# Reading 512 moving columns of the dense products one from each half row in turn, in a two-layer hybrid mixer kernel

## What is computed

```python
def sq_relu_mlp(h, w1, w2):
    return jnp.square(jax.nn.relu(h @ w1)) @ w2
...
for l in range(DEPTH):
    need_ctx = l < DEPTH - 1
    ...
    o_lat, o_ctx = hybrid_mixer(
        modulate(x, norm1_g[l], sh1, sc1), modulate(x_ctx, norm1_g[l], csh1, csc1), w_in[l], ...)
    x = x + g1 * o_lat
    x = x + g2 * sq_relu_mlp(modulate(x, norm2_g[l], sh2, sc2), w_ff1[l], w_ff2[l])
    if need_ctx:
        x_ctx = x_ctx + cg1 * o_ctx
        x_ctx = x_ctx + cg2 * sq_relu_mlp(modulate(x_ctx, norm2_g[l], csh2, csc2), w_ff1[l], w_ff2[l])
return x
```

## Time and profile before

| | |
|---|---|
| median of three executions | 1476.16 us |
| profiled execution | 1476.19 us |
| its span in the trace | 1474.4 us |
| TensorE matmul busy | 1449.2 us, 98% of the span |
| TensorE weight load busy | 1224.4 us, 83% |
| VectorE busy | 939.8 us, 64% |
| ScalarE busy | 645.3 us, 44% |
| GpSimd busy | 209.2 us, 14% |

### The profile page before, as it was taken

How to read it: one execution, slowest core, us unless ns; L and a number is a source line. 1 busy time by engine, 2 the same in 40 slices (tenths; PEclk the granted TensorE clock), 3 DMA queues, 4 the chain that set the end, 5 groups by cost and what they waited for, 6 DMA issues and landing times.

```text
span 1474.4 us, 24978 instructions
## 1 busy us (share of the span) xinstructions
PE 1449.2 (98%) x10474; PEld 1224.4 (83%) x10474; DVE 939.8 (64%) x1479; ACT 645.3 (44%) x969; POOL 209.2 (14%) x172
## 2 busy tenths in 40 slices
PE   8999999999999999999999999999999999999999
PEld 4888777776778888888888888788888779999999
DVE  5777467847445656698655554668378865675564
ACT  5722534364254434542123422562365655564462
POOL 0000001333111110221002200000002611122130
PEclk9999999999999999999999999999999999999999
DMA  9522223023243224256555556042242444455553
GB/s 383 215 87 93 89 95 152 30 98 107 72 186 126 97 86 162 99 197 225 188 190 197 187 202 202 9 144 93 94 158 91 143 137 137 170 210 189 186 197 115
DMA packets 37409, 215.07 MB, mean 146 GB/s; under 512 B 4017, under 2 KB 7729, under 8 KB 13617
## 3 DMA queue, kind: packets, MB, share of 16 engines
q1 hardware_dynamic: 37298, 213.48, 41.1%
HBM read 211.37 MB, written 2.10 MB: 145 GB/s over the span
## 4 chain that ended last, share of the span: by engine, by line
PE 90%; DVE 6%; ACT 2%; issue 1%; DMA 1%; POOL 0%; SPq 0%; DVEq 0%; ACTq 0%
PE ps L1216 11%; PE ps L1215 11%; PE ps L1214 11%; PE ps L591 10%; PE ps L593 10%; PE ps L592 10%; PE ps L814 3%; PE ps L569 2%; PE ps L602 2%; PE ps L603 2%; PE ps L604 2%; DVE arena L2410 1%; DVE parts L2031 1%; PE ps L712 1%; PE ps L796 1%
## 5 line engine op out<-in xcount | busy, mean ns | idle before, releaser
L593 PE MATMUL ps<-parts 128*128 128x512 f32 (+1 forms) x944 | 319.1, 338 | 0.0
L1216 PE MATMUL ps<-parts 128*128 128x512 f32 (+1 forms) x960 | 318.7, 332 | 0.0
L1214 PE MATMUL ps<-parts 128*128 128x512 f32 (+1 forms) x928 | 308.1, 332 | 0.0
L1215 PE MATMUL ps<-parts 128*128 128x512 f32 (+1 forms) x928 | 308.1, 332 | 0.0
L2072 DVE TENSOR_TENSOR parts<-ring,parts 128x1024 fp32r<-128x1024 f32 x124 | 150.1, 1252 | 129.9 <-ACT parts L1582 129.8
L1582 ACT ACTIVATE parts<-ring 128x1024 fp32r<-128x1024 f32 x124 | 124.8, 1053 | 235.9 <-PE ps L1216 228.5
L1216 PEld LDWEIGHTS ps<-parts 128*128 128x128 f32 x960 | 180.2, 188 | 18.6
L593 PEld LDWEIGHTS ps<-parts 128*128 128x128 f32 x944 | 177.2, 188 | 20.4
L591 PE MATMUL ps<-parts 128*128 128x512 f32 (+1 forms) x544 | 189.0, 347 | 0.9 <-ACT arena L1834 0.9
L1215 PEld LDWEIGHTS ps<-parts 128*128 128x128 f32 x928 | 174.2, 188 | 18.2
L1214 PEld LDWEIGHTS ps<-parts 128*128 128x128 f32 x928 | 174.2, 188 | 18.1
(11 more groups left out here) (323 smaller groups left out, 2458.1 us busy)
## 6 DMA issues: line engine op xcount, KB each, us to landing
ring<-in_w_ff SPq DMA_DIRECT2D x64, 1024.0 KB, 4.8
ring<-in_w_in SPq DMA_DIRECT2D x58, 1024.0 KB, 4.9
ring<-in_w_mod_rows SPq DMA_DIRECT2D x31, 1024.0 KB, 4.8
arena<-in_w_mod SPq DMA_DIRECT2D x8, 1024.0 KB, 17.5
arena<-in_w_mod_rows SPq DMA_DIRECT2D x8, 1024.0 KB, 9.4
ring<-in_w_branch SPq DMA_DIRECT2D x32, 256.0 KB, 5.2
ring<-in_w_out SPq DMA_DIRECT2D x8, 1024.0 KB, 4.9
ring<-in_w_in SPq DMA_DIRECT2D x6, 512.0 KB, 12.2
```

The lines of the kernel that those rows point to most:

```text
L593: last = pe.matmul(ps[0:m, 0:n], w_lo[:, k, c], x_hi[:, k, 0:n], start=False, stop=(k == KD - 1))
L1214: pe.matmul(ps[:, 0:nt], w_hi[:, k, c], x_hi[:, k, inner(l)], start=(k == 0), stop=False)
L1215: pe.matmul(ps[:, 0:nt], w_hi[:, k, c], x_lo[:, k, inner(l)], start=False, stop=False)
L1216: last = pe.matmul(ps[:, 0:nt], w_lo[:, k, c], x_hi[:, k, inner(l)], start=False, stop=(k == kt - 1))
```

## The change

The three helpers turn the order of a row of 512 columns; with any other width they leave it alone. `in_turns` reads column 0 of the first half, column 0 of the second half, column 1 of the first half, and so on, so that the sum in PSUM has latents and context interleaved. `from_turns` reads such a row so that the two halves come out one after the other, and `by_halves` gives the same three-dimensional form to a natural row. All split products with 512 moving columns read in turns, and so does the plain product of the ML branch. Products with 256 moving columns stay as they are, also where the new call stands in the line. Readers that keep a tile for later use put the order back; the gates, the branch products, `ACC` and the ReLU stay in the turned order, as all of them have it, and their next readers (lines 1571, 1596, 2060, 2080) put it back. No instruction is added, removed or moved, and the addresses of all tensors are the same.

```diff
+def in_turns(columns):
+
+    return columns.rearrange("p (two t) -> p t two", two=2) if columns.shape[-1] == 512 else columns
+
+
+def from_turns(columns):
+
+    return columns.rearrange("p (t two) -> p two t", two=2) if columns.shape[-1] == 512 else columns
+
+
+def by_halves(columns):
+
+    return columns.rearrange("p (two t) -> p two t", two=2) if columns.shape[-1] == 512 else columns
...
-                    pe.matmul(ps[0:m, 0:n], w_hi[:, k, c], x_hi[:, k, 0:n], start=(k == 0), stop=False)
-                    pe.matmul(ps[0:m, 0:n], w_hi[:, k, c], x_lo[:, k, 0:n], start=False, stop=False)
-                    last = pe.matmul(ps[0:m, 0:n], w_lo[:, k, c], x_hi[:, k, 0:n], start=False, stop=(k == KD - 1))
+                    hi, lo = [in_turns(x[:, k, 0:n]) for x in (x_hi, x_lo)]
+                    pe.matmul(ps[0:m, 0:n], w_hi[:, k, c], hi, start=(k == 0), stop=False)
+                    pe.matmul(ps[0:m, 0:n], w_hi[:, k, c], lo, start=False, stop=False)
+                    last = pe.matmul(ps[0:m, 0:n], w_lo[:, k, c], hi, start=False, stop=(k == KD - 1))
...
-                        last = pe.matmul(ps[0:96, :], MG_W[:, k, :], x[:, k, :], start=(k == 0 and x is M_HI[l]),
+                        last = pe.matmul(ps[0:96, :], MG_W[:, k, :], in_turns(x[:, k, :]), start=(k == 0 and x is M_HI[l]),
...
-                        pe.matmul(ps[:, :], w_hi, M_HI[l][:, k, :], start=(k == 0), stop=False)
+                        pe.matmul(ps[:, :], w_hi, in_turns(M_HI[l][:, k, :]), start=(k == 0), stop=False)
...
-                        dense(("br", l, n, m), wb, i * P, OUT[:, n % 2], 2, nt)
+                        dense(("br", l, n, m), wb, i * P, OUT[:, n % 2], 2, nt, turn=True)
...
-                        pe.matmul(ps[:, 0:nt], w_hi[:, k, c], x_hi[:, k, inner(l)], start=(k == 0), stop=False)
-                        pe.matmul(ps[:, 0:nt], w_hi[:, k, c], x_lo[:, k, inner(l)], start=False, stop=False)
-                        last = pe.matmul(ps[:, 0:nt], w_lo[:, k, c], x_hi[:, k, inner(l)], start=False, stop=(k == kt - 1))
+                        hi, lo = [in_turns(x[:, k, inner(l)]) for x in (x_hi, x_lo)]
+                        pe.matmul(ps[:, 0:nt], w_hi[:, k, c], hi, start=(k == 0), stop=False)
+                        pe.matmul(ps[:, 0:nt], w_hi[:, k, c], lo, start=False, stop=False)
+                        last = pe.matmul(ps[:, 0:nt], w_lo[:, k, c], hi, start=False, stop=(k == kt - 1))
...
-                act.activation(HID_HI[:, m % 16, inner(l)], r, ACT.Square).then_inc(*s_f1.up(("high", l, m)))
+                act.activation(by_halves(HID_HI[:, m % 16, inner(l)]), from_turns(r), ACT.Square).then_inc(*s_f1.up(("high", l, m)))
...
-                        src = ps[64 * i:64 * i + 64, :]
-                        act.activation(keys[r, 2 * j + i, :], src, ACT.Sigmoid, scale=-1.0)
-                        last = act.activation(FT[r, 2 * j + i, :], src, ACT.Sigmoid)
+                        src = from_turns(ps[64 * i:64 * i + 64, :])
+                        act.activation(by_halves(keys[r, 2 * j + i, :]), src, ACT.Sigmoid, scale=-1.0)
+                        last = act.activation(by_halves(FT[r, 2 * j + i, :]), src, ACT.Sigmoid)
...
-                dve.tensor_tensor(HID_LO[:, m % 16, inner(l)], SG[:, m % 3, 0:nt], HID_HI[:, m % 16, inner(l)], ALU.subtract)\
+                dve.tensor_tensor(by_halves(HID_LO[:, m % 16, inner(l)]), from_turns(SG[:, m % 3, 0:nt]),
+                                  by_halves(HID_HI[:, m % 16, inner(l)]), ALU.subtract)\
...
-                    last = dve.scalar_tensor_tensor(out=X[:, m, a], in0=ps[:, a],
-                                                    scalar=modv[:, l, 16 + 24 * w + m, s:s + 1], in1=x[:, m, a],
-                                                    op0=ALU.mult, op1=ALU.add)
+                    out, before = X[:, m, a], x[:, m, a]
+                    value = from_turns(ps[:, 0:nt])
+                    if l == 0:
+                        value = value[:, s]
+                    else:
+                        out, before = by_halves(out), by_halves(before)
+                    last = dve.scalar_tensor_tensor(out=out, in0=value, scalar=modv[:, l, 16 + 24 * w + m, s:s + 1],
+                                                    in1=before, op0=ALU.mult, op1=ALU.add)
```

More of the change, by code:

```diff
@@ L563, in bank, with dense @@
                 return PS[b]
-            def dense(name, w, cols, rhs, kt, n, m=P):
+            def dense(name, w, cols, rhs, kt, n, m=P, turn=False):
                 ps = bank(name)
                 for k in range(kt):
-                    last = pe.matmul(ps[0:m, 0:n], w[:, k, cols:cols + m], rhs[:, k, 0:n],
+                    x = rhs[:, k, 0:n]
+                    last = pe.matmul(ps[0:m, 0:n], w[:, k, cols:cols + m], in_turns(x) if turn else x,
                                      start=(k == 0), stop=(k == kt - 1))
@@ L601, in value_step @@
                     pe.wait_ge(*s_ml.at(("w", l, ("in", name), k // 4)))
-                pe.matmul(ps[:, 0:256], M_HI[l][:, k, t], w_hi[:, k, :], start=(k == 0), stop=False)
-                pe.matmul(ps[:, 0:256], M_HI[l][:, k, t], w_lo[:, k, :], start=False, stop=False)
-                last = pe.matmul(ps[:, 0:256], M_LO[l][:, k, t], w_hi[:, k, :], start=False, stop=(k == KD - 1))
+                hi, lo = in_turns(w_hi[:, k, :]), in_turns(w_lo[:, k, :])
+                pe.matmul(ps[:, 0:256], M_HI[l][:, k, t], hi, start=(k == 0), stop=False)
+                pe.matmul(ps[:, 0:256], M_HI[l][:, k, t], lo, start=False, stop=False)
+                last = pe.matmul(ps[:, 0:256], M_LO[l][:, k, t], hi, start=False, stop=(k == KD - 1))
                 if k == KD - 1:
@@ L716, in first_products @@
                             pe.wait_ge(*s_ml.at(("w", l, ("in", name), k // 4)))
-                        pe.matmul(ps[:, :], w_lo, M_HI[l][:, k, :], start=False, stop=False)
+                        pe.matmul(ps[:, :], w_lo, in_turns(M_HI[l][:, k, :]), start=False, stop=False)
                     if pair:
@@ L722, in first_products @@
                         w_hi = split(l, ("in", name))[0][:, k, j * P:(j + 1) * P]
-                        last = pe.matmul(ps[:, :], w_hi, M_LO[l][:, k, :], start=False, stop=(k == KD - 1))
+                        last = pe.matmul(ps[:, :], w_hi, in_turns(M_LO[l][:, k, :]), start=False, stop=(k == KD - 1))
                         if k == KD - 1:
@@ L795, in branch_parted @@
                         pe.wait_ge(*s_ml.at(("out", l, n, k)))
-                    pe.matmul(ps[:, 0:nt], w_hi[:, k, c], x_hi[:, k, 0:nt], start=(k == 0), stop=False)
-                    pe.matmul(ps[:, 0:nt], w_hi[:, k, c], x_lo[:, k, 0:nt], start=False, stop=False)
-                    last = pe.matmul(ps[:, 0:nt], w_lo[:, k, c], x_hi[:, k, 0:nt], start=False, stop=(k == 1))
+                    hi, lo = [in_turns(x[:, k, 0:nt]) for x in (x_hi, x_lo)]
+                    pe.matmul(ps[:, 0:nt], w_hi[:, k, c], hi, start=(k == 0), stop=False)
+                    pe.matmul(ps[:, 0:nt], w_hi[:, k, c], lo, start=False, stop=False)
+                    last = pe.matmul(ps[:, 0:nt], w_lo[:, k, c], hi, start=False, stop=(k == 1))
                 last.then_inc(*product.up(key))
@@ L1228, in ff_first @@
                             pe.wait_ge(*s_wlo.at((l, f, k // 4)))
-                        pe.matmul(ps[:, 0:nt], w_hi, H_HI[:, k, inner(l)], start=(k == 0), stop=False)
-                        pe.matmul(ps[:, 0:nt], w_lo, H_HI[:, k, inner(l)], start=False, stop=False)
+                        pe.matmul(ps[:, 0:nt], w_hi, in_turns(H_HI[:, k, inner(l)]), start=(k == 0), stop=False)
+                        pe.matmul(ps[:, 0:nt], w_lo, in_turns(H_HI[:, k, inner(l)]), start=False, stop=False)
                     pe.wait_ge(*s_hl.at(("hl", l, k)))
@@ L1233, in ff_first @@
                         w_hi = ff_parts(l, f)[0].rearrange("p (k c) -> p k c", k=KD)[:, k, j * P:(j + 1) * P]
-                        last = pe.matmul(ps[:, 0:nt], w_hi, H_LO[:, k, inner(l)], start=False, stop=(k == KD - 1))
+                        last = pe.matmul(ps[:, 0:nt], w_hi, in_turns(H_LO[:, k, inner(l)]), start=False, stop=(k == KD - 1))
                         if k == KD - 1:
@@ L1611, in evac @@
                         for queries, r in ((LATE, FW), (EARLY, BW)):
-                            last = act.activation(queries[r, 2 * j + i, 0:nt], ps[64 * i:64 * i + 64, 0:nt], ACT.Silu)
+                            last = act.activation(by_halves(queries[r, 2 * j + i, 0:nt]), from_turns(ps[64 * i:64 * i + 64, 0:nt]),
+                                                  ACT.Silu)
                 elif name == "hv":
@@ L2059, in merged_low @@
                     dve.wait_ge(*s_mh.at(("a", l, k)))
[L2060 removed]
+                    dve.scalar_tensor_tensor(out=by_halves(A_LO[:, k, inner(l)]), in0=from_turns(ACC[:, k, 0:nt]), scalar=0.5,
+                                             in1=by_halves(A_HI[:, k, inner(l)]),
```

(4 more changed lines are left out.)

25 lines of the change are left out of this document (13 added, 12 removed).

## The result

The changed kernel takes 1441.93 us (median of 4 runs, 1441.1 to 1442.13) against 1475.93 us (1475.16 to 1477.4) for the kernel before: a ratio of 0.9767 with an interval of 0.9751 to 0.9784. The forecast was 1442. The profiled execution took 1442.13 us, with a span of 1440.3 us against 1474.4.

What follows compares the result with a forecast made beforehand. TensorE's matmul distance was taken as the bound. Gains of 17.7 (layer 0 feed-forward), 15.4 (its mixer) and 1.9 us (first tiles, layer 1), together 35, less 1 for readers, took 1476.19 to 1442 us; 8-in-10 range 1428 to 1524.

Steps and rivals of the forecast that it cites:

- What bounds the kernel: TensorE is busy 98% of the span at full clock, so time is the number of matmuls times their distance.
- The distance: Start to start of split matmuls with 512 columns: 227 ns falls to 215.5, a gain of 11.5 ns each.
- Feed-forward part of layer 0: 1536 matmuls there gain 11.5 ns each, 17.7 us, counted in full.
- Mixer of layer 0 and first tiles: Mixer: 1576 matmuls, 18.1 us, taken at 85%, 15.4; first tiles share 1.9 us with layer 1.
- the discount of 15%: Layer 0's mixer: only 85% of 18.1 us counted, as branch steps coming back through VectorE would be late.
- Layer 1: With layer 0's first tiles, 328 matmuls worth 3.8 us, of which half, 1.9 us, was counted.
- The plain products: Plain float32 products of the ML branch, read in turns: already two cycles for each column, so costed at nothing.
- The readers: Stride-2 reads that put the order back: full rate for most, the rest covered, 1 us lost in all.
- The reason: The loss is a collision of moving-row reads with the weight load; two streams 1024 bytes apart avoid it.
- the second rival: Nothing happens: the loss is a toll of the float32r stream, one cycle per 16 columns in any order; 1476 us, chance 0.10.
- The third rival: One access for each column: changed matmuls take 430 ns, a loss of 698 us, 2174 us in all; chance 0.20.

## Why the prediction was right, and where it was not

**What bounds the kernel**: right. Time followed the distance of the matmuls' starts: the split products gave 39.0 us by it and the plain ones took 3.3 back, against 34.1 us of span.

**The distance**: 215.5 ns was forecast, 215.8 measured. The old mean was 226.7 and not 227, so a product gained 10.9 and not 11.5 ns in the feed-forward part.

**Feed-forward part of layer 0**: 17.7 forecast, 16.7 measured, all of it the 0.6 ns a product: 1536 x 10.9 = 16.7. "In full" was right.

**Mixer of layer 0 and first tiles**: 15.4 and part of 1.9 were forecast, 13.4 measured, but not for the reason given. The 1672 split products gained their full distance, 19.0 us or 11.4 each. Of this the plain products took 3.3 back, and the clock 0.8 (1.5 by its fall, less 0.7 at the start). What the discount of 15% stood for was small: TensorE's wait for VectorE's split (line 2052, before 2031) grew from 0.9 to 1.4 us, and one pause of 0.7 us came in the small products, for which the profile names no releaser.

**Layer 1**: half of its share was too little. It gained 4.0 us, of which 3.2 are distances: 96 of its 232 products had stood at 230 to 234 ns, and not at 227. Most of the rest is the clock, which fell there in the kernel before only.

**The plain products**: this is the term that was mis-sized. "they already take two cycles for each column, so I cost them at nothing" confused a rate with an independence of order: 32 x 0.11 = 3.5 us were lost, and leaving them natural gave them back.

**The readers**: 1 us in all was forecast, and none of it shows. The durations were partly wrong. In PSUM stride 2 cost nothing on either engine. In SBUF it cost ScalarE 257 ns on 633 and VectorE 124 on 762, though line 2260 had promised full rate; that row's 1218 ns already held whatever its stride cost, with no natural twin beside it. It stayed covered.

The errors cancel: 1.0 us too much in the feed-forward part and 3.3 for the plain products, against 1 us of readers that never showed and 5.0 from discounts on the other split products (17.3 forecast, 22.3 measured), of which waits and the clock took 1.6. That 1442 was hit to 0.1 us is luck.

**The reason** was wrong, though its number was right, so the hit on 216 ns was luck in part too. The loss is no collision with the weight load (narrower loads lose as much) and 1024 bytes are no condition (16 bytes do). The premise, "A loss that moves with the place and not with the number of columns", took two losses for one. The base does go with the columns, 32 cycles at 227 ns and 16 at 113, and stays at every place; the place adds 0 to 8 ns to it, which `value_step` held. Reading in turns lowered both: `value_step` fell from 120 to 112 ns, layer 1's first products from 230 to 234 down to 216. "The toll of the stream", the second rival's cause, was right about the natural order, and wrong that the order could not change it. The third rival's price is real too, for 8 and more pieces and for every stride tried. What holds in all split runs is this: the natural order loses one cycle in 16 columns at full clock, and one column of each of two lines in turn loses nothing but the 2.5 ns that the repeated column also has. No other order tried is below the natural one. Quarters lose 70 ns, halves by 2 127 and by 4 41, strides 218 to 248. That two lines are held at once fits the orders in turns and the step between 8 and 16 bytes, but not halves by 2. How the lines are fetched, and why stride 2 costs as much as stride 4, stays open: the gain of reading in turns is shown, its mechanism is not.

## What to carry to other kernels

When TensorE is busy throughout, compare the distance of starts with the number of columns over the clock: what is left over is a stall that no busy share shows, and here reading one column of each of two lines in turn removed 11 of 13.4 ns a product. Apply it to `float32r` operands alone, price it for each kind of operand from a run of that kind, and put the order back where PSUM is read, where the stride is free on ScalarE and VectorE. Try no neighbouring order by analogy: four places, runs of two or a plain stride cost 25 to 103% more than the natural order. All this was measured on one kernel and with `float32r` and float32 operands only.

## What the runs showed of the hardware that was not expected

- A `float32r` product of 512 columns follows the last after 215.8 ns in turns between two lines, 16 to 1024 bytes apart, and after 216 with one column repeated; 227 natural; 452 with stride 2.
- Plain float32 has no loss in natural order (429 ns for 1024 cycles, 426.7). It pays for alternating (540), little for stride 2 (451) and nothing for runs of four (428).
- The loss of the natural order is gone at half the granted clock: 426 to 428 ns for 512 columns, at 1.2 GHz.
- The place of the weights against the moving row adds up to 8 ns (227 to 235 ns with 512 columns, 113 to 120 with 256). Weights read at every 4th column take a product of 256 columns to 237 ns.
- With 256 columns in turns the distance is 111.6 ns with 128 weight columns and 109.2 with 96 and fewer.
- ScalarE reading 512 float32 from SBUF with stride 2 takes 890 ns instead of 633, and from PSUM 587 either way.
